# Load queues, the ones row and the norms' order in the first stage; the router in column groups; the last head's order

## The chip, the cores and the metric

One core of one Trainium2 chip runs the whole program. Its engines are TensorE (PE in the profile), VectorE (DVE), ScalarE (ACT), GpSimd (POOL) and SyncE (SP), each with its own instruction stream; PEld is TensorE's weight load. SyncE, ScalarE and GpSimd start DMAs, each in the order of its stream; the queue of an engine is written SPq, ACTq or POOLq. The metric is the time of one execution in microseconds, the median of several runs.

## The reference

Two layers over 256 latent tokens (x) and 256 context tokens (ctx), 1024 wide, all in float32. Each sublayer is `x <- LayerNorm(alpha * x + gate * f(x * (1 + scale) + shift))`, where the six modulation vectors come from `silu(c) @ w_mod + b_mod`, one set for x and one for ctx. Layer 0 mixes tokens with box means, layer 1 with a gated DeltaNet over eight heads, chunks of 64 and both directions. Both end in a mixture of 16 experts.

```python
def pool_mixer(h, w_pool, scale, rows):      # four groups of 256 columns
    outs = []
    for gi, k in enumerate(POOL_WINDOWS):    # (2, 4, 8, 16)
        ...
        outs.append(m - hg)                  # box mean over k (x k) tokens, less the token
    p = jnp.stack(outs, axis=2)
    y = jnp.einsum('blgc,gcd->blgd', p, w_pool).reshape(B, L, D)
    return y * scale

def gdn_mixer(h, w_in, conv_w, a_log, dt_bias, norm_g, w_out, init_f, init_b):
    ...                                      # projections, short convolution, gates
    o_f, s_f = gdn_chunked(q, k, v, g[0], beta[0], init_f)   # solves (I + A) in each chunk,
    ...                                      # then a recurrence over chunks
    o = o * lax.rsqrt(jnp.mean(o * o, -1, keepdims=True) + 1e-6) * norm_g.astype(f32)
    o = o * jax.nn.silu(heads(z, DN_DV))
    return o @ w_out, s_f, s_b

def moe(h, w_router, b_router, w_gate, w_up, w_down):
    scores = jax.nn.sigmoid((h @ w_router).astype(jnp.float32))
    sel = scores + b_router.astype(jnp.float32)
    ...                                      # best group of 4 experts, top 2 in it
    hid = jax.nn.silu(jnp.einsum('bld,edf->blef', h, w_gate)) * jnp.einsum('bld,edf->blef', h, w_up)
    y = jnp.einsum('blef,efd->bld', hid * combine[..., None].astype(hid.dtype), w_down)
```

## The kernel before

**Layout.** x and ctx lie in m.x, 64 tokens of each to a tile: x on partitions 0 to 63, ctx on 64 to 127 (MT = 4 tiles, KD = 8 chunks of 128 columns). The modulation products run in units: a unit is a set of weight loads of 1 MB into a ring of six slots, a step on TensorE for each (`pe_mod`, L284; in column groups of 32 rows, 128*32 in the profile), a sum with the bias on VectorE (`dve_mod`, L304), spread products that broadcast the sums to all partitions (`pe_mod_spread`), and copies by ScalarE (`act_mod`, L311). Units 0 to 5 belong to layer 0's stage; 0 and 5 have eight loads and steps, 1 to 4 four each.

**Queues of the first stage.** SyncE's stream (from L1996) issues x, ctx, two halves of the pooling matrices, unit 0's eight loads, pool_w, units 1 and 2, the rest of the constants, units 3, 4 and 5, and then the expert weights (`sp_moe_first`, 3 MB an expert). Each ring load waits for the step that frees its slot, and each bias load for the spread products of the unit two before. ScalarE's stream (from L2061) loads c, c_ctx, the early constants and pool_r, applies silu, copies the ones row, copies the pooled chunks, and behind chunk 1 issues pool_scale and the norm vectors (each broadcast to 128 partitions) and the router's weights and bias (L2074) before chunk 2's copies.

**TensorE in the first stage** (from L2104): c is transposed; `pe_ones_pooled` (L912) multiplies the four quarters of the ones row, which every later pooled shift needs; `pe_pool` (L934) pools KD chunks, with unit 0's steps between them (`beside`); then the modulation columns, unit 1, `pool_y` for four tiles with units 1 to 4 between. VectorE runs the norms of the four tiles: sums (`summed`, L346 to L354), the centred passes (`centred`, L359), the base folded in, the scaled passes (L368). The h rows are stored for the experts' gather.

**Router** (`pe_router`): h is transposed, eight products with w_router (L526) run one behind the other into rows 0 to 15 of a bank, ScalarE copies the logits (L566 in the profile), transposes bring the tokens to partitions. While the logits are taken on, TensorE runs unit 5's steps 0 to 4 (`in_router`), then 5 to 7. The experts follow, in tiles of 64 tokens: gate and up (L741), down (L753), with tokens gathered and scattered by GpSimd's DMAs.

**DeltaNet.** A loop over x from -1 to 8 overlaps heads: `pe_step`, `act_step` and `dve_step` project head x+1, invert blocks of head x on GpSimd (L1168, L1170), join and close them (L1448, L1460, L1475, L1845), and run the recurrence (L1553 to L1609). For the last head nothing is left to project, so `pe_out_early` (L1667) forms the output product of heads 0 to 5 into banks 0 to 3, while the inverted blocks come back. `dve_x` (L381, L384) applies the norm to x, and `dve_out_early` (L1690, L1694) adds the part to x. `pe_out_end` has the last two heads. The second layer's router and experts follow.

L1892 is a product of layer 1's setup that already runs in four column groups, with the same helper columns `v.add_groups`.

## Time and profile before

| | before |
|---|---|
| median of 3 runs | 985.71 us (984.33 to 988.64) |
| profiled execution | 985.4 us |
| its span | 983.5 us |
| TensorE busy, its weight loads | 80%, 48% |
| VectorE, ScalarE, GpSimd busy | 44%, 34%, 30% |
| mean granted TensorE clock | 0.879 of full speed |
| moved by DMA | 220.47 MB, mean 224 GB/s |
| chain that ended last | TensorE 47%, DMA 15%, GpSimd 13%, VectorE 10% |

The span goes from the first to the last instruction; the execution adds 1.9 us around it. Busy shares are averages over stages: the first 130 us load some 47 MB beside TensorE's work, the experts alternate between weights and products, the head loop is small operations on all engines, and the last 150 us are experts again. A row of the chain gives the start, the duration and what was running; "issue" is time in which nothing shown was awaited, and ACTq or SPq stands for the time an engine's queue took to issue a DMA. A float32 product shows as two records, so x8 are four products. Clock 1.00 is 2.4 GHz, and half clock 1.2 GHz.

### The profile page before, as it was taken

The numbers are of one execution on the slowest core, as the hardware profiler recorded it, in microseconds if no ns is written. First come the engines' busy times: TensorE is split into PE (matmuls) and PEld (weight loads), VectorE is DVE, ScalarE is ACT, GpSimd is POOL, SyncE is SP. The second block draws the span as 40 slices with busy tenths as digits, with TensorE's granted clock in tenths as the row PEclk, the third lists the DMA queues.
The fourth block names the chain that finished last, engine by engine and source line by source line (L and its number), as shares of the span: only waits on it lengthen the run. The fifth ranks groups of instructions, "written<-read, shape, count | busy, mean of one in ns | idle before, by whom it ended". The sixth has DMA issues, their size and how long they took to land.

```text
span 983.5 us, 14963 instructions
## 1 busy us (share of the span) xinstructions
PE 791.2 (80%) x5203; PEld 472.6 (48%) x5203; DVE 430.9 (44%) x1039; ACT 336.3 (34%) x776; POOL 292.1 (30%) x694
## 2 busy tenths in 40 slices
PE   5787959999996288779998999988897744999970
PEld 3343425555553035227665676665654432555540
DVE  0048444111112846126766666667563543221116
ACT  1131322222222244325645456474531121222221
POOL 0000112333233000703553835537370011333230
PEclk9798979999998688759999889899887765999995
DMA  9998999999781993585152451513210097999923
GB/s 276 396 409 314 375 380 378 367 378 329 288 315 60 391 341 80 187 261 143 20 135 44 108 130 35 137 37 115 44 46 9 11 408 300 359 383 376 391 84 127
DMA packets 115874, 220.47 MB, mean 224 GB/s; under 512 B 44631, under 2 KB 78751, under 8 KB 104801
## 3 DMA queue, kind: packets, MB, share of 16 engines
q1 hardware_dynamic: 105503, 200.97, 58.9%
q0 software_dynamic: 8224, 15.75, 4.8%
q10 hardware_dynamic: 2084, 2.92, 1.0%
q8 instruction: 39, 0.64, 0.3%
q14 instruction: 24, 0.20, 0.1%
HBM read 213.27 MB, written 17.33 MB: 234 GB/s over the span
## 4 chain that ended last, share of the span: by engine, by line
PE 47%; DMA 15%; POOL 13%; DVE 10%; issue 5%; ACT 5%; SPq 3%; ACTq 1%; DVEq 0%; POOLq 0%
PE banks L741 15%; PE banks L753 8%; POOL arena L1170 6%; POOL arena L1168 6%; DMA weight_ring<-in_w_mod_dram 4%; PE banks L1188 3%; DMA inverted_blocks<-arena 3%; PE banks L1667 3%; PE banks L722 3%; PE banks L284 3%; SPq L1141 2%; DMA arena<-blocks 2%; DMA blocks<-arena 2%; DMA arena<-h_of_tokens,row_now 2%; PE banks L934 2%
## 5 line engine op out<-in xcount | busy, mean ns | idle before, releaser
L1188 PE MATMUL banks<-h_cols,weight_ring 128*128 128x512 f32 (+1 forms) x384 | 163.9, 558 | 1.5 <-ACT modulation L311 0.7
L798 DVE TENSOR_TENSOR arena<-arena,banks 128x128 f32<-128x128 f32 x42 | 12.1, 287 | 203.2 <-ACT arena L769 203.2
L856 POOL DMA_INDIRECT y_of_tokens<-arena,place_now x42 | 44.1, 1050 | 169.0 <-ACT arena L776 169.0
L1188 PEld LDWEIGHTS banks<-h_cols,weight_ring 128*128 128x128 f32 x384 | 71.5, 204 | 40.2 <-issue 34.4
L284 PE MATMUL banks<-weight_ring,c_cols 128*32 128x512 f32 x384 | 57.9, 721 | 40.9 <-DMA weight_ring<-in_w_mod_dram 40.8
L1170 POOL TENSOR_TENSOR arena<-arena 128x60 f32<-128x60 f32 (+10 forms) x240 | 79.6, 332 | 18.8
L1168 POOL TENSOR_TENSOR arena<-arena 128x60 f32<-128x60 f32 (+10 forms) x240 | 78.1, 326 | 18.8
L834 POOL DMA_INDIRECT arena<-h_of_tokens,row_now x50 | 49.3, 985 | 91.7 <-DVE place_of_slot L703 43.5
L764 ACT COPY arena<-arena 64x1024 f32<-64x1024 f32 x46 | 48.1, 1045 | 77.5 <-PE banks L722 58.2
L741 PE MATMUL banks<-weight_ring,arena 128*64 128x256 f32 x576 | 67.8, 390 | 1.1 <-ACT arena L764 1.1
L722 PE MATMUL banks<-const,arena 64*128 64x64 f32 x352 | 57.1, 285 | 13.9 <-ACT arena L764 13.9
L722 PEld LDWEIGHTS banks<-const,arena 64*128 64x128 f32 x352 | 45.3, 198 | 36.8 <-issue 22.1
L741 PEld LDWEIGHTS banks<-weight_ring,arena 128*64 128x64 f32 x576 | 42.4, 141 | 30.6 <-issue 7.1
L1164 POOL TENSOR_TENSOR arena<-arena,const 128x256 f32<-128x256 f32 x8 | 6.2, 772 | 170.4 <-DMA arena<-blocks 170.4
L769 ACT ACTIVATE arena<-banks 128x128 f32<-128x128 f32 x42 | 11.7, 278 | 126.1 <-PE banks L741 126.1
L284 PEld LDWEIGHTS banks<-weight_ring,c_cols 128*32 128x32 f32 x384 | 10.4, 120 | 79.9 <-issue 44.2
L1229 DVE SCALAR_TENSOR_TENSOR h_rows<-arena,h_rows 128x512 f32<-128x512 f32 (+1 forms) x64 | 41.5, 648 | 1.6
L794 DVE COPY arena<-banks 128x512 f32<-128x512 f32 x44 | 30.4, 691 | 24.4 <-PE banks L722 24.4
L304 DVE TENSOR_TENSOR mod_sums<-banks,mod_sums 128x512 f32<-128x512 f32 x8 | 5.5, 682 | 70.9 <-PE banks L284 70.9
L776 ACT COPY arena<-banks 128x512 f32<-128x512 f32 x42 | 24.6, 587 | 33.3 <-PE banks L753 33.3
L753 PE MATMUL banks<-weight_ring,arena 128*64 128x512 f32 x144 | 34.9, 605 | 0.0
L1627 ACT ACTIVATE arena<-banks,arena 128x128 f32<-128x128 f32 x24 | 8.8, 368 | 67.0 <-PE banks L1571 67.0
(292 smaller groups left out, 1452.8 us busy)
## 6 DMA issues: line engine op xcount, KB each, us to landing
weight_ring<-in_w_mod_dram SPq DMA_DIRECT2D x48, 1024.0 KB, 9.3
weight_ring<-in_dn_w_in_dram SPq DMA_DIRECT2D x32, 512.0 KB, 7.3
weight_ring<-in_w_gate_dram SPq DMA_DIRECT2D x13, 1024.0 KB, 11.2
weight_ring<-in_w_up_dram SPq DMA_DIRECT2D x13, 1024.0 KB, 14.2
weight_ring<-in_w_down_dram SPq DMA_DIRECT2D x13, 1024.0 KB, 17.3
arena<-in_w_gate_dram SPq DMA_DIRECT2D x7, 1024.0 KB, 11.6
arena<-in_w_up_dram SPq DMA_DIRECT2D x7, 1024.0 KB, 15.0
arena<-in_w_down_dram SPq DMA_DIRECT2D x7, 1024.0 KB, 16.1
```

Of the source, the lines that this page charges most:

```text
L284: mm = pe.matmul(m.ps[j * COL:(j + 1) * COL, 0, :], m.c_cols[:, rows * i + k, :], w[:, k, c * BANK:(c + 1) * BANK], start=(i == 0), stop=( ...
L722: mm = pe.transpose(m.ps[:, B_TURN, k * TILE:(k + 1) * TILE], v.rows[:, k, :], v.ident[0:TILE, 0:TILE])
L741: mm = pe.matmul(column_half(B_GU, h)[:, 0:2 * P], v.slots_T[:, k, :], gate_up(slot, k)[:, :, h * P:(h + 1) * P], start=(k == 0), stop=(k ...
L753: mm = pe.matmul(column_half(B_DOWN, h), v.hidden[:, f, :], down(slot, f)[:, h * BANK:(h + 1) * BANK], start=(f == 0), stop=(f == FC - 1))
L764: act.copy(v.rows_flat, v.rows_in[u]).then_inc(s(t_ + "rows_copied"), 1)
L794: dve.tensor_copy(v.slots_T, m.ps[:, B_TURN, :].rearrange("p (k n) -> p k n", k=KD)).then_inc(s(t_ + "slots_T"), 1)
L834: pool.indirect_dma_start(v.rows_in[u], None, h_dram, bass.IndirectOffsetOnAxis(m.row_now[:, at:at + 1], 0), bounds_check=last_token, oob_ ...
L856: pool.indirect_dma_start(y_halves, bass.IndirectOffsetOnAxis(m.place_now[:, u:u + 1], 0), v.y_tile[u], None, bounds_check=last_row, oob_i ...
L1168: then(pool.tensor_tensor(part, U[:, 0:q, j:j + 1].to_broadcast([P, q, BLK - 1 - j]), M[:, j, j + 1:BLK].unsqueeze(1).to_broadcast([P, q, ...
L1170: then(pool.tensor_tensor(U[:, 0:q, j + 1:BLK], U[:, 0:q, j + 1:BLK], part, ALU.subtract))
L1188: mm = pe.matmul(bank(6 + j % 2)[:, 0:CTX + SEQ - n0], head_w[h % 2][:, j, k, :], m.hT[:, k, n0:CTX + SEQ], start=(k == 0), stop=(k == KD ...
L1229: ins = dve.scalar_tensor_tensor(out=out, in0=src, scalar=tap, in1=out, op0=ALU.mult, op1=ALU.add)
```

## The change

- **Loads.** ctx moves from SyncE's queue to ScalarE's, ahead of pool_r. pool_scale and the norm vectors move from ScalarE to SyncE, behind unit 1; the router's weights and bias behind unit 2.
- **Ones row.** Its products run inside the pooling, three behind chunk 3 and the last behind chunk 5; ScalarE copies them there. The wait for all four moves from chunk 1 to the modulation columns. pool_r counts on the semaphore of pool_m's second half.
- **Norm order.** The fourth sum and unit 3's sum (L304) come ahead of all four centred passes.
- **Router.** Four column groups of 32 columns take two chunks each, in two rounds; the logits' copy takes 128 partitions, and the transposes become products with `v.add_groups`, which add the four groups. Both routers use it.
- **Last head.** Five heads instead of six go into the early part. TensorE's join waits for the first of the part's passes, its close for the third. VectorE does the first tile's part, then the transposes, then the second tile's part. Four products of heads 5 and 6 go between the recurrence's steps, into banks 6 and 7; the head's own transposes use bank 0. `dve_x`'s four passes are spread over the steps of heads 3 to 6.

```diff
     r = 12288
-    v.logits_T = a[0:N_EXPERTS, r:r + 512]
+    v.logits_T = a[:, r:r + 512]
...
         def pe_mod_columns(pe):
             pe.wait_ge(s("mod_summed"), 1)
             pe.wait_ge(s("pooled_T"), 2 * (KD - 1))
+            pe.wait_ge(s("silu_and_ones"), 1 + NW)
...
-        def dve_x(dve, tag, n, xt, stat):
+        def dve_x(dve, tag, n, xt, stat, passes=(0, 1)):
...
+            if 0 in passes:
+                dve.scalar_tensor_tensor(out=x, in0=x, scalar=v.mean_var[:, stat, 0:1], in1=m.ln[:, 0, :], op0=ALU.subtract,
+                                         op1=ALU.mult).then_inc(s("ln_gained"), 1)
+            if 1 in passes:
+                dve.wait_ge(s("ln_gained"), c + 1)
+                dve.scalar_tensor_tensor(out=x, in0=x, scalar=v.mean_var[:, stat, 2:3], in1=m.ln[:, 1, :], op0=ALU.mult,
+                                         op1=ALU.add).then_inc(s("ln_x"), 1)
...
-            for k in range(KD):
-                mm = pe.matmul(m.ps[0:N_EXPERTS, 4, 0:L.tiles * P], v.w_router[:, k, :],
-                               m.hT[:, k, 0:L.tiles * P], start=(k == 0), stop=(k == KD - 1))
...
+            for r in range(2):
+                for g in range(4):
+                    k = 4 * r + g
+                    mm = pe.matmul(m.ps[g * COL:(g + 1) * COL, 4, 0:L.tiles * P],
+                                   m.small[:, k * N_EXPERTS:k * N_EXPERTS + COL],
+                                   m.hT[:, k, 0:L.tiles * P], start=(r == 0), stop=(r == 1))
...
             for t in range(L.tiles):
-                mm = pe.transpose(m.ps[:, 5, t * N_EXPERTS:(t + 1) * N_EXPERTS], v.logits_T[:, t * P:(t + 1) * P],
-                                  v.ident[0:N_EXPERTS, 0:N_EXPERTS])
+                mm = pe.matmul(m.ps[:, 5, t * N_EXPERTS:(t + 1) * N_EXPERTS], v.logits_T[:, t * P:(t + 1) * P],
+                               v.add_groups[:, 0:N_EXPERTS], start=True, stop=True)
...
-            act.copy(v.logits_T[:, 0:L.tiles * P], m.ps[0:N_EXPERTS, 4, 0:L.tiles * P]).then_inc(s("router_logits_T"), 1)
+            act.copy(v.logits_T[:, 0:L.tiles * P], m.ps[:, 4, 0:L.tiles * P]).then_inc(s("router_logits_T"), 1)
...
-        def pe_ones_pooled(pe):
-            pe.wait_ge(s("const"), 32)
-            for w in range(NW):
-                mm = pe.matmul(m.ps[:, (1, 2, 5, 6)[w], :], v.spread[1][0:2, :], v.ones_rows[:, w, :], start=True, stop=True)
-            mm.then_inc(s("c_turned"), 1)
-
-        def act_ones_pooled(act):
-            act.wait_ge(s("c_turned"), 2)
-            for w in range(NW):
-                act.copy(v.ones_pooled[:, w, :], m.ps[:, (1, 2, 5, 6)[w], :]).then_inc(s("silu_and_ones"), 1)
+        ONES_BANKS = (1, 2, 7, 1)
+
+        def pe_ones_pooled(pe, w):
+            if w == 0:
+                pe.wait_ge(s("pool_m_rest"), 32)
+            if w == 3:
+                pe.wait_ge(s("silu_and_ones"), 2)
+            pe.matmul(m.ps[:, ONES_BANKS[w], :], v.spread[1][0:2, :], v.ones_rows[:, w, :], start=True, stop=True
+                      ).then_inc(s("c_turned"), 1)
+
+        def act_ones_pooled(act, w):
+            act.wait_ge(s("c_turned"), w + 2)
+            act.copy(v.ones_pooled[:, w, :], m.ps[:, ONES_BANKS[w], :]).then_inc(s("silu_and_ones"), 1)
 
         def pe_pool(pe, beside):
             for c in range(KD):
                 if c == 0:
                     pe.wait_ge(s("x_loaded"), 32)
                     pe.wait_ge(s("pool_m"), 16)
-                if c == 1:
-                    pe.wait_ge(s("silu_and_ones"), 1 + NW)
                 if c == KD // 2:
-                    pe.wait_ge(s("pool_m_rest"), 16)
+                    pe.wait_ge(s("pool_m_rest"), 32)
                 if c >= 2:
                     pe.wait_ge(s("pooled_T"), 2 * (c - 1))
...
+        def turn_bank(h):
+            return 7 if h < HEADS - 1 else 0
...
-                mm = pe.transpose(bank(7)[:, t * P:(t + 1) * P], o_rows[:, t, :], v.ident)
+                mm = pe.transpose(bank(turn_bank(h))[:, t * P:(t + 1) * P], o_rows[:, t, :], v.ident)
...
-        OUT_EARLY = HEADS - 2
+            act.activation(oT[:, h, :], bank(turn_bank(h))[:, 0:SEQ], ACT.Copy, scale=norm_g).then_inc(s("out_copied"), 1)
+
+
+
+        OUT_EARLY = HEADS - 3
         out_part = m.ring[:, 2, 0:D]
 
-        def pe_out(pe, h0, h1):
-            for t in range(XT):
-                for half in range(2):
-                    for h in range(h0, h1):
-                        mm = pe.matmul(bank(2 * t + half), oT[:, h, t * P:(t + 1) * P],
-                                       w_out[h // 4][:, h % 4, half * BANK:(half + 1) * BANK],
-                                       start=(h == h0), stop=(h == h1 - 1))
-                mm.then_inc(s("dn_y"), 1)
+        def out_banks(t, end):
+            return (0, 2)[t] if not end else (6, 2)[t]
+
+        def pe_out(pe, t, half, heads, end, first, last):
+            for h in heads:
+                mm = pe.matmul(bank(out_banks(t, end) + half), oT[:, h, t * P:(t + 1) * P],
+                               w_out[h // 4][:, h % 4, half * BANK:(half + 1) * BANK], start=(h == first), stop=(h == last))
+            return mm
...
-            pe_out(pe, 0, OUT_EARLY)
+            for t in range(XT):
+                for half in range(2):
+                    mm = pe_out(pe, t, half, range(OUT_EARLY), False, 0, OUT_EARLY - 1)
+                mm.then_inc(s("dn_y"), 1)
+
+        def pe_out_beside(pe, n):
+            if n == 0:
+                pe.wait_ge(s("out_copied"), HEADS - 1)
+            half, h = divmod(n, 2)
+            pe_out(pe, 0, half, (OUT_EARLY + h,), True, OUT_EARLY, HEADS - 1)
 
         def pe_out_end(pe):
             pe.wait_ge(s("out_copied"), HEADS)
-            pe_out(pe, OUT_EARLY, HEADS)
-
-        def dve_out_early(dve):
-            for t in range(XT):
-                dve.wait_ge(s("dn_y"), t + 1)
-                dve.wait_ge(s("mod_ready"), READY_END[6] - 2)
-                if t > 0:
-                    dve.wait_ge(s("part_in_x"), 2 * t)
-                dve.tensor_tensor(out_part, dn_y(t), mod_vec(GATE1), ALU.mult).then_inc(s("part_in_x"), 1)
-                dve.wait_ge(s("part_in_x"), 2 * t + 1)
-                dve.wait_ge(s("ln_x"), MT + t + 1)
-                x = m.x[:, 2 * t, :]
-                dve.scalar_tensor_tensor(out=x, in0=x, scalar=ALPHA, in1=out_part, op0=ALU.mult, op1=ALU.add
-                                         ).then_inc(s("part_in_x"), 1)
+            for half in range(2):
+                mm = pe_out(pe, 0, half, (HEADS - 1,), True, OUT_EARLY, HEADS - 1)
+            mm.then_inc(s("dn_y"), 1)
+            for half in range(2):
+                mm = pe_out(pe, 1, half, range(OUT_EARLY, HEADS), True, OUT_EARLY, HEADS - 1)
+            mm.then_inc(s("dn_y"), 1)
...
+        def dve_out_early(dve, t):
...
+            dve.tensor_tensor(out_part, dn_y(t, False), mod_vec(GATE1), ALU.mult).then_inc(s("part_in_x"), 1)
+            dve.wait_ge(s("part_in_x"), 2 * t + 1)
...
+        X_STEP = 3
...
             if x == HEADS - 1:
-                pe.wait_ge(s("part_in_x"), 2 * XT)
+                pe.wait_ge(s("part_in_x"), 1)
             if closed(x):
                 pe_join32(pe, x)
             if made(x):
                 pe_project(pe, x + 1, 2, KD // 2, KD)
+            if x == HEADS - 1:
+                pe.wait_ge(s("part_in_x"), 3)
             if closed(x):
...
+                elif x == HEADS - 1 and 1 <= k[0] <= 4:
+                    pe_out_beside(pe, k[0] - 1)
...
             if x == HEADS - 1:
-                dve.wait_ge(s("x_moved"), 48)
-                for t in range(XT):
-                    dve_x(dve, "ln0b_", t, 2 * t, 2 * t)
-                dve_out_early(dve)
+                dve_out_early(dve, 0)
...
+            if X_STEP <= x < X_STEP + 2 * XT:
+                if x == X_STEP:
+                    dve.wait_ge(s("x_moved"), 48)
+                t, k = divmod(x - X_STEP, 2)
+                dve_x(dve, "ln0b_", t, 2 * t, 2 * t, (k,))
             if closed(x):
                 dve_turn_blocks(dve, x)
+            if x == HEADS - 1:
+                dve_out_early(dve, 1)
+            if closed(x):
                 out, p = minus_p5(dve, x, 1)
                 dve.tensor_scalar(out, p, -1.0, None, ALU.mult).then_inc(s("joined"), 1)
...
-        def dn_y(t):
-            return m.ps[:, 2 * t:2 * t + 2, :].rearrange("p a n -> p (a n)")
+        def dn_y(t, end=True):
+            n = out_banks(t, end)
+            return m.ps[:, n:n + 2, :].rearrange("p a n -> p (a n)")
...
         def _(sp):
             sp.dma_start(m.x[0:HALF, :, :], in_x[0].rearrange("(t p) d -> p t d", p=HALF)).then_inc(s("x_loaded"), 16)
-            sp.dma_start(m.x[HALF:P, :, :], in_ctx[0].rearrange("(t p) d -> p t d", p=HALF)).then_inc(s("x_loaded"), 16)
             sp.dma_start(v.pool_m[:, 0:2], in_pool_m[:, 0:2]).then_inc(s("pool_m"), 16)
             sp.dma_start(v.pool_m[:, 2:4], in_pool_m[:, 2:4]).then_inc(s("pool_m_rest"), 16)
             sp_mod(sp, 0)
             sp.dma_start(v.pool_w, in_pool_w[0].rearrange("w (c p) d -> p w c d", p=P)).then_inc(s("pool_vectors"), 16)
             sp_mod(sp, 1)
+            sp.dma_start(v.pool_scale, in_pool_scale[0].partition_broadcast(P)).then_inc(s("pool_vectors"), 16)
+            ln_loads(sp, 0, 0)
             sp_mod(sp, 2)
+            sp.dma_start(v.w_router, in_w_router.rearrange("(k p) e -> p k e", p=P)).then_inc(s("small_loads"), 16)
+            sp.dma_start(v.b_router, in_b_router.partition_broadcast(P)).then_inc(s("small_loads"), 16)
             sp.dma_start(m.const[:, EARLY:], in_const[:, EARLY:]).then_inc(s("const_rest"), 16)
             for u in (3, 4, 5):
                 sp_mod(sp, u)
@@ -2061,17 +2102,17 @@
             act.dma_start(m.c_rows[0:KD, :], in_c[0].rearrange("(k p) -> k p", p=P)).then_inc(s("c_loaded"), 16)
             act.dma_start(m.c_rows[KD:2 * KD, :], in_c_ctx.rearrange("(k p) -> k p", p=P)).then_inc(s("c_loaded"), 16)
             act.dma_start(m.const[:, 0:EARLY], in_const[:, 0:EARLY]).then_inc(s("const"), 16)
-            act.dma_start(v.ones_rows, in_pool_r.rearrange("g (w n) -> g w n", w=NW)).then_inc(s("const"), 16)
+            act.dma_start(m.x[HALF:P, :, :], in_ctx[0].rearrange("(t p) d -> p t d", p=HALF)).then_inc(s("x_loaded"), 16)
+            act.dma_start(v.ones_rows, in_pool_r.rearrange("g (w n) -> g w n", w=NW)).then_inc(s("pool_m_rest"), 16)
             act.wait_ge(s("c_loaded"), 32)
             act.activation(m.c_silu[:, :], m.c_rows[:, :], ACT.Silu).then_inc(s("silu_and_ones"), 1)
-            act_ones_pooled(act)
             for c in range(KD):
                 act_pool(act, c)
-                if c == 1:
-                    act.dma_start(v.pool_scale, in_pool_scale[0].partition_broadcast(P)).then_inc(s("pool_vectors"), 16)
-                    ln_loads(act, 0, 0)
-                    act.dma_start(v.w_router, in_w_router.rearrange("(k p) e -> p k e", p=P)).then_inc(s("small_loads"), 16)
-                    act.dma_start(v.b_router, in_b_router.partition_broadcast(P)).then_inc(s("small_loads"), 16)
+                if c == 3:
+                    for w in range(3):
+                        act_ones_pooled(act, w)
+                if c == 5:
+                    act_ones_pooled(act, 3)
...
             pe.wait_ge(s("silu_and_ones"), 1)
-            pe.wait_ge(s("const"), 32)
+            pe.wait_ge(s("const"), 16)
             pe.transpose(m.ps[:, 7, 0:2 * KD], m.c_silu[:, :], v.ident[0:2 * KD, 0:2 * KD]).then_inc(s("c_turned"), 1)
-            pe_ones_pooled(pe)
             pe.wait_ge(s("columns"), 3)
 
             def beside(steps):
                 for u, i in steps:
                     pe_mod(pe, u, i)
-            pe_pool(pe, lambda c: beside([(0, i) for i in ((), (), (0,), (1,), (2, 3), (4,), (5,), (6, 7))[c]]))
+
+            def in_pool(c):
+                beside([(0, i) for i in ((), (), (0,), (1,), (2, 3), (4,), (5,), (6, 7))[c]])
+                for w in {3: (0, 1, 2), 5: (3,)}.get(c, ()):
+                    pe_ones_pooled(pe, w)
+            pe_pool(pe, in_pool)
...
             dve_fold_gain(dve, SCALE2, v.spare, READY_END[2], 32)
-            for t in range(3):
-                centred(t)
             summed(3)
             dve_mod(dve, 3)
-            centred(3)
+            for t in range(MT):
+                centred(t)
```

## Rows read from the trace of the kernel before

**Rows 1.** Chain of waits of the first 131 us (start us, us, what)

```profile
11.77 7.01 PE banks L912 x8
18.78 5.48 PE banks L934 x32
26.13 10.09 ACTq L2074
...
46.63 1.93 PE banks L934 x16
...
51.48 1.90 PE banks L284 x16
...
106.52 7.05 PE banks L526 x16
...
115.71 4.41 PE banks L284 x38
```

**Rows 2.** Stretches: us, PE, PEld, DVE, ACT, POOL busy, clock, DMA share, GB/s

```profile
6.00:12.00 6.00, 0.49 (x2) 0.52 (x3) 0.17 (x1) 0.00 (x0) 0.00 (x0) 1.00 1.04 204
15.00:42.00 27.00, 19.83 (x109) 11.70 (x111) 0.00 (x0) 5.19 (x14) 0.00 (x0) 0.83 1.02 418
43.00:47.00 4.00, 4.00 (x36) 2.04 (x30) 0.00 (x0) 0.65 (x2) 0.00 (x0) 1.00 1.18 316
84.00:99.00 15.00, 8.54 (x58) 2.23 (x61) 12.72 (x17) 1.28 (x3) 0.00 (x0) 0.77 0.74 271
222.00:226.00 4.00, 3.88 (x31) 2.42 (x29) 1.14 (x3) 0.84 (x2) 2.17 (x4) 1.00 0.70 159
```

**Rows 3.** DMA issues at 2.3, 100.0, 127.0 us (KB each, us to landing)

```profile
arena<-in_pool_m_dram SPq DMA_DIRECT2D x1, 1024.0 KB, 15.1
...
weight_ring<-in_w_mod_dram SPq DMA_DIRECT2D x1, 1024.0 KB, 14.3
...
weight_ring<-in_w_down_dram SPq DMA_DIRECT2D x1, 1024.0 KB, 25.1
```

**Rows 4.** Timeline of TensorE: start us, us, what, [idle before <-releaser]

```profile
157.79 3.62 PE L741 MATMUL banks<-weight_ring,arena 128*64 128x256 f32 x32
...
826.17 6.22 PE L741 MATMUL banks<-weight_ring,arena 128*64 128x256 f32 x32 [1.13 <-ACT arena L764]
```

**Rows 5.** Timeline of VectorE, around 94 us

```profile
93.73 0.67 DVE L304 TENSOR_TENSOR mod_sums<-banks,mod_sums 128x512 f32<-128x512 f32 x1
```

**Rows 6.** Timeline of SyncE's queue

```profile
210.90 10.71 SPq L1113 DMA_DIRECT2D dn_inputs<-in_dn_dt_bias_dram  x1
```

**Rows 7.** Chain of waits at 359 and at 797 us

```profile
359.50 1.90 PE banks L1892 x16
...
797.24 5.30 PE banks L526 x16
```

**Rows 8.** Chain of waits, last head

```profile
724.88 20.62 PE banks L1667 x48
...
745.52 1.24 DVE weight_ring L1690
...
749.80 1.08 PE banks L1460 x32
...
750.90 0.44 DVE arena L1845
...
766.68 0.36 DVE arena L1607
...
774.44 6.54 PE banks L1667 x8
```

**Rows 9.** Timeline of ScalarE and VectorE, last head

```profile
742.74 1.64 ACT L1489 COPY arena<-arena 32x256 f32<-32x256 f32 x4 [6.93 <-DMA arena<-inverted_blocks]
...
747.92 1.78 DVE L1448 STREAM_TRANSPOSE arena<-arena 32x256 f32<-32x256 f32 x4
```

**Rows 10.** Waits of VectorE in 570 to 575 us, third head

```profile
DVE arena L1448 <- DMA arena<-inverted_blocks: 1.4, 1, 1.4
```

14 lines of the change are left out of this document (8 added, 6 removed).

## The prediction

> **What bounds the kernel now.** The page's shares of the chain average stages with different limits, so I went stage by stage. In the chain of waits over the first 131 us [rows 1] the reader sees one limit after another: the ones row's eight records (L912, 7.01 us), the pooling (L934), ScalarE's queue held for 10.09 us at the issue of L2074, the pooling's end at 51.48 + 1.90 = 53.4 us, the router product (L526, 7.05 us), steps of the modulation products (L284, 4.41 us). Beside it runs the DMA stream [rows 2]: 418 GB/s in 15 to 42 us, but 204 in 6 to 12 and 271 in 84 to 99. So the first stage has two limits close together, and what an edit takes off the engines counts only as far as the weights come earlier too. The expert tiles behind it follow each other on TensorE; the third expert's last weight lands at 127.0 + 25.1 = 152.1 us [rows 3] and is first wanted at 157.8 [rows 4]. The head loop goes by GpSimd's inversion until the last head (part 3).
>
> **Part 1, the DMA stream of the first stage.** Three things change it.
> (a) x goes to partitions 0 to 63 and ctx to 64 to 127, now one behind the other in SyncE's queue, later from two queues. While they load, 204 GB/s flow instead of 418 [rows 2]: 2.1 MB take 10.3 us and would take 5.0 at the full rate. The trace has no two such halves side by side, so the gain lies between 0 (they share the halved rate) and 5.3 us (they add up). Neither end is nearer to a row; I take the middle, 2.6.
> (b) In 84 to 99 us the stream loses 15 x (1 - 271/418) = 5.3 us [rows 2], since SyncE waits for ring slots and for the spread products, and these for L304 at 93.73 [rows 5]. The new order puts the fourth norm sum and this L304 ahead of the three centred passes, and all before it comes earlier, so SyncE's waits end while older loads are in flight. 5.3 us gained; bounds 3 and 5.3.
> (c) The router's 64-byte rows move onto SyncE's queue, ahead of the constants and unit 3. Beside a second queue's loads they cost 4 x (1 - 316/418) = 1.0 us in 43 to 47 us. The nearest case of small rows alone on SyncE's queue is 222 to 226 us: 4 x (1 - 159/418) = 2.5 us [rows 2]. So 1.5 us are lost; bounds 0 and 2.5. SyncE will be held at the b_router issue as ScalarE was; at L1113 such a hold took it 10.71 us [rows 6] and the stream thinned only behind it. The loads of unit 2 in flight cover it.
> Together the stream runs 2.6 + 5.3 - 1.5 = 6.4 us earlier at the expert weights.
>
> The Trainium skill speaks against (a): "SBUF — State Buffer", section "Can I just issue two DMAs to hit both halves?", says that concurrent transfers to the two halves serialize, with only 6% over one. The trace agrees that one half alone runs at half the rate (204 against 418 GB/s); no run here shows two. By that rule the sum would be about 2.3 us worse; it is the first rival.
>
> **Part 2, the engines of the first stage.** ScalarE's hold goes: TensorE idles some 8 us in it and falls to half clock (0.83 over 15 to 42 us [rows 2]). L912's four products, in 7.01 us at half clock before any pooling, become four of about 0.86 us between pooling chunks. TensorE then waits for x, ctx and the first pool_m (landed at 2.3 + 15.1 = 17.4 us [rows 3]). From a start at about 15: two chunks 5.5 us as now, six at 1.93, eight modulation steps at 0.95, the ones row 3.4, in all 28 us [rows 1]. The pooling ends near 43 instead of 53.4 us, and VectorE's chain behind it gains about the same. Its new order adds a wait: L304 for unit 3 stands ahead of all four centred passes and the scaled ones, and unit 3's weights land about when it comes up; I allow 1 to 2 us, about what the idle before L403 costs now, which goes. pool_scale now arrives behind unit 1 and pool_y waits for it, about 1 us, counted in. The router product in column groups is two rounds instead of eight; L1892 has this shape and takes 1.90 us [rows 7], so 7.05 - 1.90 = 5.1 us go. The logits' copy and the products that add the groups have the same free sizes as before and cost nothing more.
> But all this meets the stream. Next on TensorE behind the logits stand unit 5's steps 0 to 4; the fifth weight landed at 100.0 + 14.3 = 114.3 us [rows 3], and TensorE finished the steps at 120.1 [rows 1]. The step behind the landing could have ended at 115.3, so there are 4.8 us of slack. The new landing is 6.4 us earlier, less 1.2, because the four stores of h (2.1 MB) now come wholly before it: 109.1. TensorE, freed from hold and router, would be there by about 105. So the gain is 4.8 + 6.4 - 1.2 = 10.0 us and not the 15 of the engines alone; most of the router's 5.1 us is hidden here. Gather and tiles behind it shift unchanged: the third expert lands at 152.1 - 6.4 = 145.7 and is wanted at 147.8. **Stage 1: -10.0 us**, bounds -5 (halves serialize, small rows at their worst, idle half refilled) and -14 (halves add up).
>
> **Part 3, the last head.** Before, L1667 runs 24 products, 20.62 us to 745.5 [rows 8]; VectorE does two passes of 1.24 us, then its four transposes (1.78 us [rows 9]), and TensorE joins at 749.80; the DVE pass behind that ends at 751.3 [rows 8]. After: 20 products (17.2 us) end at 742.1, but the inverted blocks arrive at 742.7, when ScalarE's copy starts with them [rows 9]. Transposes to 744.5, the second pair of early passes 2.5, the pass that releases the close 0.44: 747.5. That is 3.9 us earlier (bounds 2 and 5). The passes of L381 and L384 move to heads 3 to 6, 1.28 us in each; VectorE waits there at least 1.4 us for the blocks [rows 10], which hides them; without that cover they would cost 5.1.
> Four products go between the recurrence's steps. Such a product takes 20.62/24 = 0.86 us at full and 6.54/4 = 1.64 at half clock; the DVE pass that TensorE awaits there takes 0.36 [rows 8]. Two at either clock cost 2 x 1.28 + 2 x 0.50 = 3.6; TensorE idles less there, and in the records full clock returns behind its busy stretches, which I put at 1.2 back: +2.4, bounds +0.5 and +5. At the end the first token tile needs 2 products instead of 4, but the second ends behind the same eight as before, and only the 0.6 us between their end and VectorE's next sum go. **Last head: -3.9 + 2.4 - 0.6 = -2.1 us**, bounds -5 and +2.
>
> **Part 4, the second router.** L526 takes 5.30 us [rows 7], the first half of its records at half clock. Two rounds at half clock are 1.8 us, with nothing beside them: **-3.5 us**, bounds -3.2 and -4.4.
>
> Sum: -10.0 - 2.1 - 3.5 = -15.6. The profiled execution took 985.4 us (span 983.5), close to the median of 985.71. Forecast **969.8 us**.
>
> **Rivals.**
> 1. The halves serialize: (a) is 0, 969.8 + 2.6 = 972.4. For it: no row shows the full rate while half-height loads are the bulk. Against: none of them had both halves in flight together. Chance 0.22.
> 2. The halves add up and unit 5's loads follow without a gap: 969.8 - 2.7 - 1 = 966. Chance 0.13.
> 3. The fills stay at half clock and cost 6 instead of 2.4: 973.4. For it: most of this recurrence now runs at half clock. Against: TensorE idles less there than before. Chance 0.13.
> 4. The change does not do what it says: the hold moves with the small loads and drains the stream for its 10 us, ahead of unit 3. Stage 1 gives nothing: 979.8. Against: [rows 2, 6], where only the 4 us behind the hold were thin. Chance 0.05.
> 5. Slower: tokens are routed before their weights are there. It decides once the path's gain in stage 1 outruns the stream's by over 147.8 - 145.7 = 2.1 us more than forecast: TensorE then waits at each expert and falls to half clock, where the first product group of a tile takes 6.22 instead of 3.62 us [rows 4]. Eight tiles so cost 21 us; with stage 1's gain lost too, 969.8 + 10 + 21 = 1001. Against: the slack grows behind the third expert. Chance 0.03.
> The forecast itself has 0.44.
>
> **Range and chances.** The forecast and cases 1 to 3 hold 0.92. The bounds (stage 1 -14 to -5, last head -5 to +2, router -4.4 to -3.2) reach from 962 to 979; all at one end is unlikely, so 962.5 to 977.5, which leaves out cases 4 and 5. About 0.5% is what a measurement of this kernel can tell from no change. Faster by over 0.5% (below 980.8): 0.92; within 0.5%: 0.05; slower: 0.03.
>
> **What the changed profile would show.** (a) right: over 300 GB/s in 6 to 12 us and the first L934 by 15 us; wrong: first L934 at 17. (b) no stretch of 5 us under 350 GB/s in 70 to 110 us. (c) SyncE held some 10 us at b_router, thin for at most 3 us behind it. Pooling ends near 43 us; the router product takes 1.9 us, and behind it TensorE waits for unit 5's weights until about 109; the first expert tile comes 10 us earlier. Last head: the close starts 3 us behind the join, the recurrence is 2 us longer. Second router product 1.8 us. The prediction is wrong if the first tile is not 7 to 13 us earlier, or if TensorE waits for weights between expert tiles.

## The result and the profile after

| | before | after |
|---|---|---|
| median | 985.94 us (984.33 to 988.64, 4 runs) | 968.44 us (966.4 to 972.01, 4 runs) |
| profiled execution | 985.4 us | 969.0 us |
| its span | 983.5 us | 967.2 us |
| mean granted clock | 0.879 | 0.882 |

The ratio is 0.9831, 95% interval 0.9802 to 0.986: 17.5 us less, where 15.9 (985.7 to 969.8) had been forecast. The time was right. The parts were not: the first stage gave about half of what was forecast or less, the last head three to four times as much.

The page of after, its span, the engines' row and its rows by slice of the span:

```profile
span 967.2 us, 14976 instructions
PE 778.0 (80%) x5209; PEld 468.9 (48%) x5209; DVE 430.1 (44%) x1039; ACT 336.4 (35%) x776; POOL 287.7 (30%) x694
...
PEclk9899979999998588859999898898977956999995
...
GB/s 246 393 360 407 423 364 393 364 374 329 300 325 33 385 337 119 201 263 94 63 148 19 135 56 98 134 33 140 44 45 12 12 409 356 357 378 386 380 73 127
```

A slice is 24 us. The third (48 to 73 us) moves less than before (360 against 409 GB/s on the page of before), the fourth more (407 against 314): the stream lost up to and behind the pooling's end and gained in the norms.

Where the 16.3 us of span went is read by laying both timelines side by side at fixed operations, start in before and after:

| operation | before | after | difference |
|---|---|---|---|
| first pooling product | 18.7 | 23.2 | +4.5 |
| modulation columns (pooling over) | 54.1 | 55.3 | +1.2 |
| router's first transpose, layer 0 | 100.5 | 99.5 | -1.1 |
| second expert tile | 147.5 | 143.7 | -3.8 |
| first head's join | 451.6 | 448.7 | -2.9 |
| seventh head's join | 700.7 | 696.3 | -4.5 |
| last head's join | 749.8 | 736.0 | -13.8 |
| router's first transpose, layer 1 | 792.7 | 779.1 | -13.6 |
| first expert tile, layer 1 | 823.9 | 807.8 | -16.1 |

These are single executions. Other kernels with the same first stage tell how far one can be trusted: the second expert tile stands at 147.5 and 149.6 us in before and e5, and at 140.7 to 144.0 us (mean 142.7) in the four with the stage of after (after, r_after, e4, f2). By the means the stage gave 5.8 us, by the table 3.8.

The same stretches as [rows 2] (columns as there):

```profile
6.00:12.00 6.00, 0.00 (x0) 0.00 (x0) 0.00 (x0) 0.00 (x0) 0.00 (x0) 1.00 1.04 270
15.00:42.00 27.00, 18.76 (x110) 11.70 (x114) 0.00 (x0) 4.99 (x13) 0.00 (x0) 0.90 1.01 374
43.00:47.00 4.00, 4.00 (x33) 1.91 (x26) 0.00 (x0) 0.65 (x2) 0.00 (x0) 0.97 0.93 305
84.00:99.00 15.00, 10.30 (x76) 3.06 (x74) 14.76 (x20) 1.48 (x4) 0.00 (x0) 1.00 1.03 411
```

The idle of 84 to 99 us is gone (411 instead of 271 GB/s). But 15 to 42 us, the best stretch of before, fell from 418 to 374. The reason shows in DMA issues at 2.2 us (KB, us to landing) and in TensorE's timeline of after:

```profile
x_rows<-in_ctx_dram ACTq DMA_DIRECT2D x1, 1024.0 KB, 21.0
...
23.24 6.86 PE L943 MATMUL banks<-arena,x_rows 64*128 64x256 f32 x48 [10.75 <-DMA x_rows<-in_ctx_dram]
...
105.42 1.92 PE L533 MATMUL banks<-h_cols,small 128*32 128x512 f32 x16 [0.73 <-ACT h_cols L571]
...
119.87 1.94 PE L284 MATMUL banks<-weight_ring,c_cols 128*32 128x512 f32 x8 [0.61 <-DMA weight_ring<-in_w_mod_dram]
122.36 1.06 PE L284 MATMUL banks<-weight_ring,c_cols 128*32 128x512 f32 x8 [0.55 <-DMA weight_ring<-in_w_mod_dram]
```

On ScalarE's queue ctx needed 21 us to land, and TensorE stood 10.75 us for it. The router product takes 1.92 us, as forecast. Then TensorE goes by the weights: the last two of unit 5. In before it did not. There it ran unit 5's steps without a wait, and the places' product behind them stood for VectorE's end of the router's chain. The same product in before and in after:

```profile
127.93 1.13 PE L554 MATMUL banks<-arena 128*64 128x36 f32 x32 [1.83 <-DVEq L686]
```

```profile
123.35 1.13 PE L562 MATMUL banks<-arena 128*64 128x36 f32 x32
```

So the shorter router product counts in the first stage until unit 5's last weight ends later than that chain.

The last head of after, in the chain of waits:

```profile
739.17 0.18 PE banks L1484
...
746.40 0.36 DVE arena L1616
...
748.03 1.71 PE banks L1680 x2
...
750.26 0.86 PE banks L1680 x2
...
762.49 8.85 PE banks L1680 x16
```

L1680 is L1667 of [rows 8]. The close (L1484) follows the join at 735.97 by 3.2 us, as forecast. Of the fills in the recurrence only the first is at half clock (1.71), the next is at full (0.86).

And one view that the prediction had not opened: GpSimd's timeline beside VectorE's in the last head. Before, GpSimd first, VectorE below:

```profile
727.15 0.33 POOL L1168 TENSOR_TENSOR arena<-arena 128x35 f32<-128x35 f32 x1
727.55 1.12 POOL L1170 TENSOR_TENSOR arena<-arena 128x35 f32<-128x35 f32 x1
728.75 1.22 POOL L1168 TENSOR_TENSOR arena<-arena 128x28 f32<-128x28 f32 x1
730.05 1.13 POOL L1170 TENSOR_TENSOR arena<-arena 128x28 f32<-128x28 f32 x1
731.25 1.22 POOL L1168 TENSOR_TENSOR arena<-arena 128x21 f32<-128x21 f32 x1
732.55 0.24 POOL L1170 TENSOR_TENSOR arena<-arena 128x21 f32<-128x21 f32 x1
...
727.28 1.28 DVE L381 SCALAR_TENSOR_TENSOR x_rows<-x_rows,small,ln_vectors 128x1024 f32<-128x1024 f32 x1
728.59 1.28 DVE L384 SCALAR_TENSOR_TENSOR x_rows<-x_rows,small,ln_vectors 128x1024 f32<-128x1024 f32 x1
729.79 1.28 DVE L381 SCALAR_TENSOR_TENSOR x_rows<-x_rows,small,ln_vectors 128x1024 f32<-128x1024 f32 x1
731.11 1.28 DVE L384 SCALAR_TENSOR_TENSOR x_rows<-x_rows,small,ln_vectors 128x1024 f32<-128x1024 f32 x1
```

and the same GpSimd operations after:

```profile
722.95 0.26 POOL L1179 TENSOR_TENSOR arena<-arena 128x35 f32<-128x35 f32 x1
723.28 0.23 POOL L1177 TENSOR_TENSOR arena<-arena 128x28 f32<-128x28 f32 x1
723.59 0.24 POOL L1179 TENSOR_TENSOR arena<-arena 128x28 f32<-128x28 f32 x1
723.91 0.22 POOL L1177 TENSOR_TENSOR arena<-arena 128x21 f32<-128x21 f32 x1
```

Beside each of `dve_x`'s four passes of 1.28 us one GpSimd operation took 1.1 to 1.2 us instead of 0.22 to 0.26, and each of the four ended about 0.1 us behind the pass beside it. That is 3.7 us of the inversion, and the inversion sets when the blocks come back. In their new places the passes met none of it: in after the first runs from 569.3 to 570.6 us, and GpSimd's inversion of that head had ended at 563.4.

### The profile page after: what moved, and what is told of

It is laid out like the page before. It is cut to its first block and busy times, and to the rows that moved or that the text cites. A ratio compares the mean times of both kernels' runs of the same rounds, so it can differ in the third digit from the quotient of the medians.

```text
span 967.2 us, 14976 instructions
## 1 busy us (share of the span) xinstructions
PE 778.0 (80%) x5209; PEld 468.9 (48%) x5209; DVE 430.1 (44%) x1039; ACT 336.4 (35%) x776; POOL 287.7 (30%) x694
## 5 line engine op out<-in xcount | busy, mean ns | idle before, releaser
L1179 POOL TENSOR_TENSOR arena<-arena 128x60 f32<-128x60 f32 (+10 forms) x240 | 77.1, 321 | 18.8
L1177 POOL TENSOR_TENSOR arena<-arena 128x60 f32<-128x60 f32 (+10 forms) x240 | 76.0, 317 | 18.8
L730 PE MATMUL banks<-const,arena 64*128 64x64 f32 x352 | 57.1, 285 | 14.9 <-ACT arena L772 14.9
L284 PEld LDWEIGHTS banks<-weight_ring,c_cols 128*32 128x32 f32 x384 | 10.3, 120 | 82.7 <-issue 42.2
L304 DVE TENSOR_TENSOR mod_sums<-banks,mod_sums 128x512 f32<-128x512 f32 x8 | 5.5, 682 | 71.8 <-PE banks L284 71.8
## 6 DMA issues: line engine op xcount, KB each, us to landing
weight_ring<-in_w_down_dram SPq DMA_DIRECT2D x13, 1024.0 KB, 17.5
arena<-in_w_down_dram SPq DMA_DIRECT2D x7, 1024.0 KB, 16.1
```

The source lines that it names most:

```text
L284: mm = pe.matmul(m.ps[j * COL:(j + 1) * COL, 0, :], m.c_cols[:, rows * i + k, :], w[:, k, c * BANK:(c + 1) * BANK], start=(i == 0), stop=( ...
L730: mm = pe.transpose(m.ps[:, B_TURN, k * TILE:(k + 1) * TILE], v.rows[:, k, :], v.ident[0:TILE, 0:TILE])
L1177: then(pool.tensor_tensor(part, U[:, 0:q, j:j + 1].to_broadcast([P, q, BLK - 1 - j]), M[:, j, j + 1:BLK].unsqueeze(1).to_broadcast([P, q, ...
L1179: then(pool.tensor_tensor(U[:, 0:q, j + 1:BLK], U[:, 0:q, j + 1:BLK], part, ALU.subtract))
```

## Experiments

The kernels ran in three groups, each with before beside them: e1, e2, e4 and e5 (before 983.88 us); r_after, f1, f2 and e7 (985.16); e3, e6, e8 and g1 (984.53). The changed kernel was run again in the second group, as r_after: 968.49 us (966.49 to 972.11, 6 runs), ratio to before 0.9824 (0.9797 to 0.9851), as expected below. Differences "to the changed kernel" are to this median. For e1, e3, e4 and e8 that goes across groups.

> The changed kernel itself, run beside the next three so that they can be compared on one chip. Both theories: 966 to 969 us, a ratio to before of 0.980 to 0.985; the start of the pooling, which goes by ctx's landing, may lie anywhere from 21 to 25 us.

### ctx on the second queue

**e1_ctx_sync, f1_ctx_sync**: ctx back in SyncE's queue, the same kernel in two groups.

```diff
+            sp.dma_start(m.x[HALF:P, :, :], in_ctx[0].rearrange("(t p) d -> p t d", p=HALF)).then_inc(s("x_loaded"), 16)
...
-            act.dma_start(m.x[HALF:P, :, :], in_ctx[0].rearrange("(t p) d -> p t d", p=HALF)).then_inc(s("x_loaded"), 16)
```

> The changed kernel with one load put back: ctx again in SyncE's queue behind x. Theory A (a half-height load on a second queue runs slowly beside SyncE's loads and holds them back; in the changed kernel ctx landed at 23.2 us and 255 GB/s flowed from 10 to 20 us): the first L943 comes at about 17.5 instead of 23.2 us, 15 to 20 us shows over 400 GB/s, the pooling ends near 49 instead of 54.5 us, and since unit 5's last weight lands 1.6 to 3 us earlier, the whole is 2 to 4 us faster than the changed kernel, 964.5 to 966.5. Rival (the weight stream's end does not depend on it): the pooling is 5 us earlier and the total stays within 1 us of 968.4.

> The same kernel as e1_ctx_sync (ctx back in SyncE's queue), now with more rounds beside the changed kernel. Theory A: 2 to 4 us faster than the changed kernel (first expert tile 3 to 5 us earlier; some of it is given back where clock states differ). Rival: within 1 us of it.

Measured: 965.99 us (964.75 to 970.24), ratio 0.982 (0.9765 to 0.9874), and 965.26 us (963.31 to 972.41), ratio 0.982 (0.9783 to 0.9858). That is 2.5 and 3.2 us below the changed kernel by medians; the intervals of the ratios overlap (two of f1's six runs lay at 972), so the size is uncertain, and the whole alone would not show it. The traces of f1 and, in the last line, of the changed kernel in the same group show where it comes from:

```profile
15.00:20.00 5.00, 2.48 (x12) 2.21 (x14) 0.00 (x0) 0.00 (x0) 0.00 (x0) 1.00 1.02 423
...
17.52 6.89 PE L943 MATMUL banks<-arena,x_rows 64*128 64x256 f32 x48 [6.53 <-DMA arena<-in_pool_m_dram]
```

```profile
15.00:20.00 5.00, 0.00 (x0) 0.00 (x0) 0.00 (x0) 0.00 (x0) 0.00 (x0) 1.00 1.02 288
```

The pooling starts at 17.5 instead of 22.2 us, the columns come at 48.0 instead of 53.2, the second expert tile at 138.6 instead of 144.0. In e1 that tile stands at 139.4, and in the four traces with ctx on ScalarE's queue nowhere earlier than 140.7.

**e2_ctx_alone**: the kernel before with ctx on ScalarE's queue, ahead of pool_r, and nothing else.

```diff
-            sp.dma_start(m.x[HALF:P, :, :], in_ctx[0].rearrange("(t p) d -> p t d", p=HALF)).then_inc(s("x_loaded"), 16)
...
+            act.dma_start(m.x[HALF:P, :, :], in_ctx[0].rearrange("(t p) d -> p t d", p=HALF)).then_inc(s("x_loaded"), 16)
```

> The kernel before with the one edit that ctx goes onto ScalarE's queue ahead of pool_r. Theory A: x and ctx do not add up, ctx lands at about 23 instead of 14.9 us, pooling starts there, and the whole is 1.5 to 5 us slower, 987 to 991. Rival (forecast's term a, 0 to 5.3 us gained): pooling starts by 17.4, 980.5 to 986.

Measured: 988.46 us (10 runs) beside 983.88 of before, ratio 1.0041 (1.0016 to 1.0065): 4.6 us slower by medians. ctx landed at 22.1 us, as theory A has it. But the pooling began only at 30.0: pool_r stands behind ctx in ScalarE's queue, so the ones row waited too, until 22.8 us, and ran its 7.2 us ahead of the pooling. The edit alone costs time; how much of the 4.6 us is ctx and how much the ones row is not shown.

**e3_halves**: SyncE issues nothing behind x until both halves have landed.

```diff
             sp.dma_start(m.x[0:HALF, :, :], in_x[0].rearrange("(t p) d -> p t d", p=HALF)).then_inc(s("x_loaded"), 16)
+            sp.wait_ge(s("x_loaded"), 32)
```

> The changed kernel, but SyncE issues nothing behind x until x and ctx have both landed, so that the two half-height loads run on two queues with nothing but the small constants beside them. If they serialize or share one half's rate: 195 to 220 GB/s from 3 us on, both landed between 12 and 14 us. If they add up: about 400 GB/s, both landed by 9 us. The time of the whole is not the question; pool_m comes later than in the changed kernel's queue.

The stretches of its trace while x and ctx load:

```profile
5.00:7.00 2.00, 0.00 (x0) 0.00 (x0) 0.00 (x0) 0.23 (x1) 0.00 (x0) 1.00 0.97 195
7.00:9.00 2.00, 0.00 (x0) 0.00 (x0) 0.00 (x0) 0.00 (x0) 0.00 (x0) 1.00 1.07 171
9.00:11.00 2.00, 0.02 (x1) 0.06 (x1) 0.00 (x0) 0.00 (x0) 0.00 (x0) 1.00 1.05 173
11.00:13.00 2.00, 0.23 (x1) 0.12 (x1) 0.18 (x1) 0.00 (x0) 0.00 (x0) 1.00 1.04 211
```

x landed at 9.7 us, ctx at 15.7. So 195 and 171 GB/s flowed with both in flight, and up to 211 with ctx alone (11 to 13 us): they do not add up, and ctx came no sooner than in one queue (14.9). The pooling began at 20.9, earlier than in the changed kernel (23.2 and 22.2 us), although SyncE had issued nothing for 15 us. So two things are apart: the halves share one half's rate, and SyncE's other loads beside ctx hold it back further (20.0 and 21.0 us to landing with them, 13.6 without). The whole took 970.28 us in the one run, which says nothing on its size.

### The loads' hold, the norms, the router

**g1_loads_sync**: the kernel before with pool_scale, the norm vectors and the router's rows on SyncE's queue.

```diff
             sp_mod(sp, 1)
+            sp.dma_start(v.pool_scale, in_pool_scale[0].partition_broadcast(P)).then_inc(s("pool_vectors"), 16)
+            ln_loads(sp, 0, 0)
             sp_mod(sp, 2)
+            sp.dma_start(v.w_router, in_w_router.rearrange("(k p) e -> p k e", p=P)).then_inc(s("small_loads"), 16)
+            sp.dma_start(v.b_router, in_b_router.partition_broadcast(P)).then_inc(s("small_loads"), 16)
...
-                if c == 1:
...
-                    ln_loads(act, 0, 0)
...
```

> The kernel before with only the loads of pool_scale, the norm vectors and the router's rows moved from ScalarE's to SyncE's queue; ctx, the ones row, the norms, the router and the last head stay as before. The forecast's step (the hold of 10 us in the pooling goes): L943's third chunk starts at 30 instead of 37 us, the pooling ends near 47 instead of 53.4 us, the router's transposes come 5 to 7 us earlier, and with 4.8 us of slack to the weights the whole is 3.5 to 6 us faster than before. Rival (the hold moves to SyncE and drains the stream): no gain, or up to 3 us slower.

Measured: 981.83 us (12 runs) beside 984.53, ratio 0.9967 (0.9943 to 0.999): 2.7 us faster, under what was expected. Its trace has the columns at 44.9 instead of 54.1 us, 9.3 us earlier, but then:

```profile
47.05 1.38 PE L284 MATMUL banks<-weight_ring,c_cols 128*32 128x512 f32 x8 [1.73 <-DMA weight_ring<-in_w_mod_dram]
49.52 1.94 PE L284 MATMUL banks<-weight_ring,c_cols 128*32 128x512 f32 x8 [1.09 <-DMA weight_ring<-in_w_mod_dram]
```

TensorE waits for unit 1's weights, and 5.5 us are left at the second expert tile. Of these 2.6 more are gone by the first head's join. That stretch takes from 302.7 to 306.9 us over the fourteen traces without an edit in it, so this part is not settled. SyncE's hold was 12.76 us here (5.03 in after). The stream did not drain in it (409 GB/s in 60 to 65 us); behind it 65 to 70 us showed 302 GB/s, about 1.4 us of the stream at 418.

**e8_norm_old**: the changed kernel with three centred passes ahead of the fourth sum and of unit 3's sum, as before.

```diff
+            for t in range(3):
+                centred(t)
             summed(3)
             dve_mod(dve, 3)
-            for t in range(MT):
-                centred(t)
+            centred(3)
```

> The changed kernel with the old order of the norms: three centred passes ahead of the fourth sum and of unit 3's sum. By the forecast's step (b): unit 3's sum, unit 5's bias loads and so its weights come 3.5 us later, the stream shows a stretch of 3 us or more under 150 GB/s around 90 to 98 us again, and the whole is 2 to 5 us slower than the changed kernel, 970.5 to 973.5. Rival (what ends last there is TensorE and VectorE's chain, not the weights): the router's transposes come at the same time and the whole moves by less than 1 us.

Measured: 973.9 us (970.61 to 976.29, 6 runs), ratio 0.988 (0.9847 to 0.9913): 5.4 us slower than the changed kernel, a little over the range. Its trace has the idle back, 95 to 100 us at 147 GB/s where r_after had 374, with unit 5's second weight issued at 98.2 instead of 94.3 us. The weights behind it bound the stage. But its second expert tile comes at 146.4 us, only 2.4 to 2.7 behind r_after and after; the rest of the 5.4 us is not placed.

**e6_router** (before with the router in column groups) and **e7_router_undone** (after without them): the router's part of the diff alone, and its reverse.

```diff
-            for k in range(KD):
-                mm = pe.matmul(m.ps[0:N_EXPERTS, 4, 0:L.tiles * P], v.w_router[:, k, :],
...
+            for r in range(2):
+                for g in range(4):
...
+                    mm = pe.matmul(m.ps[g * COL:(g + 1) * COL, 4, 0:L.tiles * P],
...
```

> The kernel before with only the router in column groups. The forecast's reading (what the first layer's product gives is mostly hidden behind unit 5's weights): 3 to 5 us faster than before. Theory D (the first layer's counts in full, since the product also holds back the steps that free ring slots, and the stream runs dry behind it: 276 and 261 GB/s in 110 to 120 us where the old product stands in the changed kernel, 414 and 433 without it): 6.5 to 9 us faster than before.

> The changed kernel with the old router product (eight products one behind the other) in both layers. The forecast's reading (in layer 0 most of the 5.1 us are hidden, since TensorE waits for unit 5's weights behind it; in layer 1 nothing hides them): the second layer's product takes 3.5 to 5.3 us instead of 1.9 and the whole is 2.5 to 4.5 us slower than the changed kernel. Rival (the first layer's counts in full too): 5.5 to 8 us slower.

e6 measured 980.07 us (12 runs) beside 984.53, ratio 0.9948 (0.9916 to 0.9981): 4.5 us faster, as the forecast read it. In its trace the stretch from the product to the places' product (L554) is 1.8 us shorter in layer 0, since TensorE now stands for unit 5's last two weights as in after, and 0.8 us to the second expert tile; layer 1's from the transposes to the first tile is 3.4 us shorter. e7 measured 977.05 us (974.41 to 978.61), ratio 0.9909 (0.988 to 0.9937): 8.6 us slower than the changed kernel, beyond both ranges and nearer to the rival's. By medians the same edit is worth about twice as much in the changed kernel; the intervals of the two differences overlap. Stretches of e7's trace behind the long product:

```profile
110.00:115.00 5.00, 4.33 (x22) 1.20 (x24) 0.64 (x4) 2.87 (x5) 0.00 (x0) 1.00 0.67 276
115.00:120.00 5.00, 5.00 (x56) 2.55 (x48) 3.19 (x21) 0.29 (x1) 0.00 (x0) 1.00 0.75 261
```

After had 414 and 433 there. With the stream running without gaps, unit 5's steps behind the product free their ring slots too late, and the loads stop. That much of theory D is there. That the gap costs time is not shown, for TensorE did not wait for a weight behind it:

```profile
121.79 2.78 PE L284 MATMUL banks<-weight_ring,c_cols 128*32 128x512 f32 x24
126.40 1.13 PE L559 MATMUL banks<-arena 128*64 128x36 f32 x32 [1.83 <-DVEq L691]
```

What ends last in e7 is the router's chain, as in before. From the product to the second expert tile e7 takes 42.7 us, after and r_after 38.3 and 39.5, so 3.2 to 4.4 us count in layer 0, and 2.8 in layer 1 (from the transposes to the first tile, against r_after). The other 1.4 to 2.6 us of the 8.6 lie in the expert and head loops between, which vary by as much from trace to trace, and stay open.

### The last head

**e4_x_last** (after, `dve_x` back in the last head) and **e5_x_spread** (before, `dve_x` spread over heads 3 to 6):

```diff
             if x == HEADS - 1:
+                dve.wait_ge(s("x_moved"), 48)
+                for t in range(XT):
+                    dve_x(dve, "ln0b_", t, 2 * t, 2 * t)
                 dve_out_early(dve, 0)
...
-            if X_STEP <= x < X_STEP + 2 * XT:
...
-                dve_x(dve, "ln0b_", t, 2 * t, 2 * t, (k,))
```

> The changed kernel with the four passes of dve_x back in the last head, ahead of its first part's passes. Theory B (such passes on VectorE slow GpSimd's steps beside them: in the trace of before L1168/L1170 over 28 and 21 columns took 1.1 to 1.2 us beside them, in that of after 0.23): the last six or seven steps of the inversion take 1.1 us again, the blocks come back 4 to 5 us later, and the whole is 3.5 to 6 us slower than the changed kernel, 972 to 974.5. Rival (the forecast's view: VectorE has 6 us of idle there, so the passes are free and the blocks come when they come): 968 to 969.5.

> The kernel before with dve_x's four passes spread over the steps of heads 3 to 6 and nothing else. Theory B: the inversion of the last head ends 4 to 5 us earlier, but TensorE's 24 products and the second pair of VectorE's passes then stand between the blocks and the join, so only 0 to 2 us come through: 984 to 986. Rival (the inversion is the bound, the order is not): 4 to 5 us, 981 to 982.

e4 measured 972.88 us (971.35 to 973.61), 4.4 us slower than the changed kernel. GpSimd's timeline of e4, beside the four passes that now run from 716.28 to 721.46:

```profile
716.15 0.35 POOL L1177 TENSOR_TENSOR arena<-arena 128x55 f32<-128x55 f32 x1
716.58 1.16 POOL L1179 TENSOR_TENSOR arena<-arena 128x55 f32<-128x55 f32 x1
717.82 1.23 POOL L1177 TENSOR_TENSOR arena<-arena 128x60 f32<-128x60 f32 x1
719.13 1.16 POOL L1179 TENSOR_TENSOR arena<-arena 128x60 f32<-128x60 f32 x1
720.37 1.24 POOL L1177 TENSOR_TENSOR arena<-arena 128x54 f32<-128x54 f32 x1
721.69 0.29 POOL L1179 TENSOR_TENSOR arena<-arena 128x54 f32<-128x54 f32 x1
```

Other operations of the inversion than in before, since the passes come at another point; the same four of 1.2 us. A fifth of 1.25 us, at 723.82, stands beside the pass of `dve_out_early` with two SBUF inputs. Then VectorE waits:

```profile
736.43 1.78 DVE L1457 STREAM_TRANSPOSE arena<-arena 32x256 f32<-32x256 f32 x4 [11.48 <-DMA arena<-inverted_blocks]
```

VectorE idles 11.5 us before the transposes, and still the passes ahead of that idle cost time. e5's times scattered (982.49 to 1112.28, 4 runs) and give no ratio, so the verdict rests on its trace. The inversion is 4 us shorter and the blocks come at 738.0, but VectorE is elsewhere then:

```profile
742.53 1.22 DVE L1692 TENSOR_TENSOR weight_ring<-banks,modulation 128x1024 f32<-128x1024 f32 x1 [7.82 <-PE banks L1669]
743.79 1.22 DVE L1696 SCALAR_TENSOR_TENSOR x_rows<-x_rows,weight_ring 128x1024 f32<-128x1024 f32 x1
744.93 1.78 DVE L1450 STREAM_TRANSPOSE arena<-arena 32x256 f32<-32x256 f32 x4
```

24 products and the second pair of passes stand ahead of the transposes, so nothing of it shows at the join. Thirteen traces together, in us (f2, below, has an order of its own):

| last head | traces | inversion | seventh join to last | seventh join to layer 1's router |
|---|---|---|---|---|
| neither | before, g1, e6, e2 | 28.0 to 28.7 | 44.9 to 49.1 | 86.7 to 92.0, mean 89.3 |
| `dve_x` spread alone | e5 | 24.4 | 46.4 | 89.4 |
| order alone | e4 | 28.4 | 44.5 | 89.5 |
| both | after, r_after, e1, f1, e7, e8, e3 | 23.7 to 24.4 | 39.2 to 40.1 | 82.5 to 83.0, mean 82.7 |

To layer 1's router each alone shows no gain, and together they give 6.6 us between the means. There were two limits one behind the other. In before the blocks lay ready at 742.7 us, but VectorE came to the transposes only at 747.9, behind TensorE's 24 products and its own passes; so earlier blocks alone give nothing. In e4 TensorE's 20 products ended at 731.0, but the blocks came at 736.4; so the new order alone gains little at the join. There TensorE idled 7.3 us, the granted clock behind the join was about 0.5, and from the recurrence's start to the output's end e4 took 27.7 us where the last row has 25.6 to 26.1.

The sizes are less sure than the signs. The first row's stretch to the last join goes with the granted clock of its first 20 us: 44.9 us at 1.00 (e2), 49.1 at 0.72 and 0.60 (before, the longest of its row; an L1188 group of eight records took 3.52 us there behind the seventh join, and 1.89 ahead of it). So the 9.2 us between before and after are chance in part. Against e2 alone both edits give 4.1 us (86.7, and 82.6 and 82.5 in e1 and f1, at the same clock).

**f2_six_early**: the changed kernel with `OUT_EARLY = HEADS - 2` and no products beside the recurrence.

```diff
-        OUT_EARLY = HEADS - 3
+        OUT_EARLY = HEADS - 2
...
-                mm = pe_out(pe, 0, half, (HEADS - 1,), True, OUT_EARLY, HEADS - 1)
+                mm = pe_out(pe, 0, half, range(OUT_EARLY, HEADS), True, OUT_EARLY, HEADS - 1)
...
-                elif x == HEADS - 1 and 1 <= k[0] <= 4:
-                    pe_out_beside(pe, k[0] - 1)
```

> The changed kernel with six heads again in the early part and no products beside the recurrence; the waits and VectorE's order stay. By the forecast's sizes: 24 products end 3.4 us later than 20 and set the join, the recurrence is 2.4 us shorter, the end part 0 to 0.6 us longer: 1 to 1.6 us slower than the changed kernel. Theory C (the fills cost only about 0.5 us, since the recurrence with them keeps the full clock, as 17.0 against 16.5 us from its start to the end part in the two profiles says): 3 to 4 us slower than the changed kernel, 971 to 972.

Measured: 970.62 us (967.54 to 973.64), ratio 0.9852 (0.9822 to 0.9882): 2.1 us slower than the changed kernel by medians, between the two expectations, and its interval overlaps that of the changed kernel. Its trace: the last stretch of the table 84.0 us (1.3 more), and from the recurrence's start to the output's end 25.4 us where the last row's have 25.6 to 26.1. So the four fills cost about 0.5 us, in kernels where TensorE idled 2.7 us at most ahead of the join.

## Why the prediction was right, and where it was not

The time was right by luck, because two wrong terms met: by the traces the first stage gave 3.8 us (5.8 between means) instead of 10.0, and the last head 9.2 (6.6 between means) instead of 2.1. The second router gave 2.5 us to the first tile instead of 3.5. By the prediction's own sign it was wrong: the first tile was to be 7 to 13 us earlier, and it is 4.5 (140.3 and 135.8).

**Part 1 (a), wrong in sign.** The bounds were 0 and 5.3, with "neither end nearer". Both assumed that only x and ctx meet. But SyncE's queue behind x holds pool_m and the ring's weights, and these run beside ctx. x landed at 9.6, pool_m's first half at 14.5, ctx at 23.2. The rows that I had (204 GB/s with one half) could not exclude a loss, so a bound below nothing belonged there. The first rival, that the halves serialize, holds (e3), and so does the section of the Trainium skill cited in the prediction: 195 and 171 GB/s with both in flight, against 204 for one. But its price was wrong too: it put (a) at nothing gained, and e1 and f1 put the edit at 2.5 and 3.2 us lost in the whole. At the second expert tile it is more, 4.3 us (e1 against after) and 5.4 (f1 against r_after), 3.7 between the means. Without (a) the sum had -7.4 for the first stage, and e1 and f1 stand 8.1 and 8.8 us ahead of before there: nearly all of the first stage's miss is this one term. The Trainium skill has the missing piece, "DMA: Bandwidth & Descriptors", section "Queues, rings and completion order": each DMA engine goes round the queues that have work, packet by packet. The landings agree with this, though no run here shows single packets.

The stream itself can be added up in stretches of 5 us, as the difference to before in us at 418 GB/s. After stood 1.6 us behind at 25 us (ctx), 4.4 behind at 75, and 2.1 to 2.4 ahead from 100 to 115, where 6.4 had been forecast.

**(b), right for the stream.** 84 to 99 us went from 271 to 411 GB/s, 5.0 us of stream, where 5.3 had been put. Without the order the changed kernel is 5.4 us slower (e8), of which its trace shows 2.4 to 2.7 in this stage. The sign given (no stretch of 5 us under 350 GB/s in 70 to 110 us) failed in one stretch, 324 in 70 to 75.

**(c), right in size where it can be seen.** SyncE was held at b_router 12.76 us in g1, and 1.4 us of stream were lost behind it. In after the hold was 5.03 us, and 65 to 70 us behind it ran at 417 GB/s; but from 25 to 75 us after lost 2.8 us of stream to before, against the 1.5 of this term, and what of it is the small loads is not shown.

**Part 2, right in its mechanism, late in its start.** The hold on ScalarE went, and alone it brings the pooling's end forward 9.3 us (g1). The pooling was to start at 15 and take 28 us, to 43; it started at 23.2 and took 31, to 54.5, over two stretches at 0.64 and 0.68 of the clock (35 to 45 us), which the sum had not priced. The prediction read L912's 7.01 us in before as half clock; its products have twice the length (1.75 instead of 0.86 us), but the granted clock over them reads 1.00, so why they were long is not shown. The router product is 1.92 us as said. The sum then went by unit 5's fifth weight (114.3 before, 109.1 forecast). It landed at 112.8, but neither kernel went by it: before went by the router's chain (L554 above), after by the eighth weight (124.3 before, 122.3 after), so the stream came 2 us earlier and not 6.4. Of after's 3.8 us at the second tile only 1.1 were there ahead of the router; 2.7 came with it. "Most of the router's 5.1 us is hidden" holds in the kernel before (e6: 0.8 to 1.8 us counted) and not in the one after (e7: 3.2 to 4.4).

**Part 3, the step that failed: "the inverted blocks arrive at 742.7".** The blocks' arrival was taken as fixed while `dve_x` was costed as moved time on VectorE ("VectorE waits there at least 1.4 us, which hides them"). That is true of VectorE. It is GpSimd that these passes had held up, 1.2 us for each. I looked at the passes' cover in the new place, not at what they cost in the old one; the row at 728.75 would have told. The Trainium skill states it, "SBUF — State Buffer", section "Who interferes with whom": a VectorE instruction with two SBUF inputs contends with a GpSimd instruction that reads SBUF, and the later one blocks until the first is done. `dve_x` reads x and the norm vectors, and the trace agrees: operations of 1.12 to 1.22 us beside passes of 1.28, each ending about 0.1 us behind its pass. The close 3 us behind the join was right. The fills were priced at 2.4 and cost 0.5: from the recurrence's start to the end part it is 17.0 us instead of 16.5. In before the products were at half clock until about 766, in after only in the first 4 us of the recurrence; so about 3 us came back, where 1.2 had been put. From the recurrence's start to the output's end 26.5 us became 25.8, where 1.8 more had been forecast. So of the 7.1 us that the last head gave beyond the forecast, 4.1 lie at the join, 2.5 in the recurrence and the output, and 0.5 behind. The third rival (the fills stay at half clock) did not come in after; in e4, where TensorE idled 7.3 us ahead of the join, that stretch took 1.9 us longer.

**Part 4, nearly right.** 5.30 became 1.98 us (1.8 forecast); from the transposes to the first tile 31.2 became 28.7, so 0.9 us of the product's 3.3 were lost behind it. The 5.30 were not fixed either: in e2 and g1 the old product took 3.6 us there.

## What to carry to other kernels

A sum that comes out right is no proof of its terms: compare term by term with the traces. When work is moved, read two views, what it hides behind in its new place and what ran slowly beside it in its old one; another engine's rows of unusual length are the sign. And where one limit stands behind another, test edits in pairs: at layer 1's router `dve_x` alone and the new order alone showed no gain, both gave 4.1 to 6.6 us. Before a term is read off two traces, look at how far traces of kernels that are alike there lie apart: 3.3 us at the second expert tile, 5.3 in the last head. The best kernel here was the changed one with ctx back on SyncE's queue, 965.3 to 966.0 us.

## What the runs showed of the hardware

- VectorE passes of 1024 columns with two SBUF inputs made a GpSimd operation of 0.23 to 0.35 us last 1.1 to 1.25 us each, four beside four passes of `dve_x`, in before, e2, e4, e6 and g1 (inversion 28.0 to 28.7 us) and not in the others (23.7 to 24.4).
- Two 1 MB loads onto partitions 0 to 63 and 64 to 127 from two queues ran at 171 to 195 GB/s together (e3), no faster than one (204 and 211); in before loads onto all 128 ran at 418.
- A 1 MB half-height load (64 partitions) on a second queue beside a full first queue landed 19.4 (f2) to 21.0 us (after) after its issue, against 13.3 to 13.7 in one queue. All loads together then ran at 256 (after) to 296 GB/s (e4) in 10 to 20 us; with one queue they ran at 199 to 248 until 15 us and at 421 to 429 from there.
